# Two weight tiles instead of one follow each normed tile in five stages of a two-block model on one core

## The chip, the cores and the metric

The kernel runs on one core of a Trainium2 chip. The metric is the device time of one launch in microseconds (us). In three runs it was 3197.97, 3209.4 and 3214.88 us, median 3209.4.

## The reference, cut to what matters

A first block of two layers works on 256 context tokens and 512 latent tokens of width 1024 (a Hyena and mLSTM mixer, then latent attention, each followed by a convolved feed-forward); a second block (attention with a state-space mixer, then a mixture of experts) works on the 512 latent tokens. What the change touches are five products that follow an RMS norm:

```
y = xf * lax.rsqrt(jnp.mean(xf * xf, axis=-1, keepdims=True) + RMS_EPS)
...
u_ctx = h_ctx @ w_in                          # mixer of layer 0
...
g, u = jnp.split(h @ w_up, 2, axis=-1)        # feed-forward of either layer
...
return jnp.split(h @ w_down, [MLA_Q_RANK, MLA_Q_RANK + MLA_KV_RANK], axis=-1)
...
proj = h @ w_in[l]                            # second block, its q and k part
```

## The kernel before

Activations lie transposed: 8 tiles of 128 features (`DT` = 8, index `kk`) by 768 tokens, split in segments of 256 and 512 (`SEGS`), or 512 tokens alone (`SEG_LAT`). Every product is made in three passes (`three_passes`, lines 301 to 306): each float operand is split into a high part rounded to fp32r and a low part, and the matmuls high by high (L304), high by low (L305) and low by high (L306) are added in PSUM. So a weight tile of 128 output features takes 24 matmuls of 512 tokens, and 24 more of 256 tokens where there is context.

A weight tile comes through a `Stream` of two slots: SyncE loads it into `raw[s]`, ScalarE rounds the high part (`high`, L279), VectorE makes the low part (`low`, L283) and raises `ready[s]`. There is one pair of parts for each slot. So the high part of the tile after next can be written only when the product of this slot's tile is finished (`product[s]`), and this product needs `ready[s]` of its own tile and `taken[s]`, which says that its PSUM area has been read out. The work goes in turns of two tiles, p = 0 and p = 1. Turn 0 is written out by `from_first` and `in_spans`, the others are a hardware loop.

Five stages begin with a norm:

1. the Hyena projection (`project_conv`, 12 weight tiles, 768 tokens), called stage 1 below
2. the first feed-forward up (`ffn_up`, 22 tiles of gate and up side by side, 768 tokens), stage 2
3. the attention down projection (`project_act`, 6 tiles, 768 tokens), stage 3
4. the second feed-forward up (`ffn_up`, 22 tiles, 512 tokens), stage 4
5. the q and k projection of the second block (`project_act` with `NormOfNorm`, 6 tiles, 512 tokens), stage 5

The norm comes out tile by tile. For each kk VectorE scales x (L426, or L598 in stage 5), ScalarE applies gain and shift and rounds (L407 and L411, or L574 and L577), and VectorE makes the low part (L433, or L605) and raises `ready` of the norm. In stage 5 VectorE then writes x itself anew with 8 instructions of L611. In `project_as_normed` TensorE waits for each kk and runs the matmuls of one weight tile on it, both segments: tile p = 0 of turn 0 in stages 1, 3 and 5, and the gate half of tile p = 0 in stages 2 and 4. After the eighth normed tile comes the rest with `project`: all of tile p = 1 in stages 1, 3 and 5, the up half of tile p = 0 in stages 2 and 4 (p = 1 follows after it). `project` goes through all kk of a segment before the next segment.

After a product, ScalarE first rounds the slot's next weights (L279), then reads PSUM: L975 in `project_conv`, L1080 in `ffn_up`, L1552 in `project_act`. In `project_conv` VectorE then adds the outer taps out of PSUM (L1005, four instructions for each weight tile) and raises `taken`; in `project_act` L1552 raises it; in `ffn_up` the product of gate and up (L1122) does.

Of the kernel before, what the change touches and what calls it, by code (L numbers as in the profile page):

```python
# [31 lines left out]
P = 128  # L32
D = 1024
DT = D // P
# [266 lines left out]
def three_passes(k, out, stationary, moving, start, stop, **more):  # L301

    (sh, sl), (mh, ml) = stationary, moving
    k.nc.tensor.matmul(out, sh, mh, start=start, stop=False, **more)  # L304
    k.nc.tensor.matmul(out, sh, ml, start=False, stop=False, **more)  # L305
    return k.nc.tensor.matmul(out, sl, mh, start=False, stop=stop, **more)  # L306
# [26 lines left out]
            turn(i, False)  # L333


def project_as_normed(k, pe, norm, parts, psum_of, segs, col=0, width=P):

    for kk in range(DT):
        pe.wait_ge(norm.ready, kk + 1)
        at = kk * width + col  # L340
        for s, (t0, n) in enumerate(segs):
            last = three_passes(k, psum_of(s), [w[:, at:at + P] for w in parts], k.h_pair.tokens(kk, t0, t0 + n),
                                kk == 0, kk == DT - 1)
    return last


class Norm:
# [560 lines left out]
def project_conv(k, weights, dst, conv_w, conv_b, silu, taps=3, segs=SEGS, norm=None, then=None, also=(), begun=False):  # L908
    nc = k.nc
    k.stage()  # L910
    norm = Norm(k, *norm, segs, k.pair(2), k.bank(6), 7, begun) if norm else None
    stream = weights if isinstance(weights, Stream) else Stream(k, weights, D)
    tiles, turns = stream.tiles, stream.tiles // 2
    t0 = segs[0][0]
    product, taken = [k.sem("product0"), k.sem("product1")], [k.sem("taken0"), k.sem("taken1")]
    middle, summed, extra = k.sem("middle"), k.sem("summed"), k.sem("extra")
    offsets = [o - taps // 2 for o in range(taps) if o != taps // 2]
    per_tile = len(offsets) * len(segs)

    def sums(n, p):  # L920

        return k.arena[:, stream.at - (p + 1) * T:stream.at - p * T][:, t0:T] if silu else dst[:, n, :]

    with k.block() as block:
        @block.sync
        def _(sp):
            if also and not stream.ahead:
                stream.begin(sp)
            for place, array in also:
                sp.dma_start(place, array).then_inc(extra, 16)  # L930
            stream.load(sp, bool(also))
            if also:
                sp.wait_ge(extra, 16 * len(also))
            if then:
                then.begin(sp, stream)

        @block.tensor
        def _(pe):
            if norm:
                norm.sum_and_spread(pe)  # L940
            elif not stream.ahead:
                keep_running(k)

            def turn(i, first):
                for p in range(2):
                    psum_of = lambda s: k.pair(p)[:, segs[s][0]:segs[s][0] + segs[s][1]]
                    pe.wait_ge(stream.ready[p], i + (stream.base + 1))
                    pe.wait_ge(taken[p], i + 1)
                    if norm and first and p == 0:
                        last = project_as_normed(k, pe, norm, stream.parts[p], psum_of, segs)  # L950
                    else:
                        last = project(k, stream.parts[p], DT, k.h_pair, psum_of, segs)
                    last.then_inc(product[p], 1)

            from_first(pe, turns, turn)

        @block.scalar
        def _(act):
            if norm:
                norm.square(act)  # L960
            for p in range(0 if stream.ahead else 2):
                stream.high(act, p, 1)
            if norm:
                norm.shift(act)

            def turn(i, last):
                for p in range(2):
                    n = 2 * i + p
                    act.wait_ge(product[p], i + 1)
                    if not last:  # L970
                        stream.high(act, p, i + 2)
                    elif then:
                        then.high(act, p, 1)
                    bias = k.col(conv_b, n) if conv_b else 0.0
                    nc.scalar.activation(sums(n, p), k.pair(p)[:, t0:T], ACT.Identity,  # L975
                                         scale=k.col(conv_w, n + tiles * (taps // 2)), bias=bias).then_inc(middle, 1)
                    if silu:
                        act.wait_ge(summed, per_tile * (n + 1))
                        nc.scalar.activation(dst[:, n, :], sums(n, p), ACT.Silu)

            in_turns(act, turns, turn)

        @block.vector
        def _(dve):
            free_all(dve, taken)
            if norm:
                norm.add(dve)
            for p in range(0 if stream.ahead else 2):
                stream.low(dve, p, 1)
            if norm:  # L990
                norm.scale(dve)

            def turn(i, last):
                for p in range(2):
                    n = 2 * i + p
                    if not last:
                        stream.low(dve, p, i + 2)
                    elif then:
                        then.low(dve, p, 1)
                    dve.wait_ge(middle, n + 1)  # L1000
                    for m, o in enumerate(offsets):
                        for a, w in segs:
                            lo, hi = max(a, a - o), min(a + w, a + w - o)
                            out = sums(n, p)[:, lo - t0:hi - t0]
                            nc.vector.scalar_tensor_tensor(out=out, in0=k.pair(p)[:, lo + o:hi + o],  # L1005
                                                           scalar=k.col(conv_w, n + tiles * (o + taps // 2)), in1=out,
                                                           op0=ALU.mult, op1=ALU.add).then_inc(summed, 1)
                        dve.wait_ge(summed, per_tile * n + len(segs) * (m + 1))
                    nc.vector.sem_inc(taken[p], 1)

            in_turns(dve, turns, turn)
# [3 lines left out]
def ffn_up(k, layer, hidden, scratch, segs, norm, then, beside=None):  # L1015
    nc = k.nc
    k.stage()
    norm = Norm(k, *norm, segs, k.pair(3), k.bank(6), 5)
# [15 lines left out]
    with k.block() as block:  # L1034
# [6 lines left out]
        @block.tensor  # L1041
        def _(pe):
            norm.sum_and_spread(pe)

            def turn(i, kind):
                for p in range(2):
                    pe.wait_ge(stream.ready[p], i + (stream.base + 1))
                    pe.wait_ge(taken[p], i + 1)
                    gate_of = lambda s: gate(p, *segs[s])
                    up_of = lambda s: up(p)[:, segs[s][0]:segs[s][0] + segs[s][1]]  # L1050
                    if kind == "first" and p == 0:
                        project_as_normed(k, pe, norm, stream.parts[p], gate_of, segs, 0, 2 * P)
                    else:
                        project(k, stream.parts[p], DT, k.h_pair, gate_of, segs, 0, 2 * P)
                    project(k, stream.parts[p], DT, k.h_pair, up_of, segs, P, 2 * P).then_inc(product[p], 1)
                    if kind in ("sum both", "sum one"):
                        beside.sum(pe, i, p, kind == "sum both")

            in_spans(pe, ((0, 1, "first"),) + (((1, 2, ""), (2, 6, "sum both"), (6, 10, "sum one"), (10, turns, "")) if beside else ((1, turns, ""),)), turn)
# [429 lines left out]
def project_act(k, weights, dst, func, bias, segs, kt=DT, x=None, norm=None, then=None, also=(), first_norm=False):  # L1489
# [11 lines left out]
    with k.block() as block:  # L1501
# [12 lines left out]
        @block.tensor  # L1514
        def _(pe):
            if norm:
                norm.sum_and_spread(pe)
            elif not stream.ahead:
                keep_running(k)

            def turn(i, first):
                for p in range(2):
                    psum_of = lambda s: k.pair(p)[:, segs[s][0]:segs[s][0] + segs[s][1]]
                    pe.wait_ge(stream.ready[p], i + (stream.base + 1))
                    pe.wait_ge(taken[p], i + 1)
                    if norm and first and p == 0:
                        last = project_as_normed(k, pe, norm, stream.parts[p], psum_of, segs)
                    else:
                        last = project(k, stream.parts[p], kt, x, psum_of, segs)
                    last.then_inc(product[p], 1)  # L1530

            from_first(pe, turns, turn)

# [2277 lines left out]
```

## Time and profile before

| what | value |
|---|---|
| runs | 3197.97, 3209.4, 3214.88 us |
| span of the profiled execution | 3207.9 us |
| PE busy | 2924.0 us, 91% |
| DVE busy | 1710.8 us, 53% |
| ACT busy | 1207.4 us, 38% |
| mean granted TensorE clock | 0.957 |

No time is given for the profiled execution besides its span, from the first to the last instruction. PE is TensorE, DVE VectorE, ACT ScalarE, PEclk the granted TensorE clock with 1.00 for 2.4 GHz and 0.50 for 1.2 GHz. A share of busy time is a mean over all stages; what holds TensorE in one of them is read from the rows of that stretch.

### The profile page before, as it was taken

What the parts mean: (1) busy time and instruction counts of PE and PEld (TensorE: products, weight loads), DVE (VectorE), ACT (ScalarE), POOL (GpSimd) and SP (SyncE); (2) the same over time, 40 slices, a digit from 0 to 9 for tenths busy, and PEclk for the clock granted to TensorE, in tenths of its full rate; (3) what the DMA queues carried; (4) which work ended last, traced back from release to release, by engine and by line L of the source; (5) the groups of instructions that cost most, each with busy time, mean ns of one, the idle gap of its engine ahead of it and who ended that gap; (6) DMA issues with size and microseconds to landing.
All of it is one profiled execution on the core that took longest, in us unless ns stands there. A gap on an engine that the chain in (4) does not pass through costs nothing. (4 is left out here: it accounts for less than half of the span.)

```text
span 3207.9 us, 37971 instructions
## 1 busy us (share of the span) xinstructions
PE 2924.0 (91%) x14246; PEld 2331.5 (73%) x14246; DVE 1710.8 (53%) x2417; ACT 1207.4 (38%) x1619; POOL 166.6 (5%) x127
## 2 busy tenths in 40 slices
PE   7999989799999899898999999989878899899996
PEld 3774777678888798675777887867745677777775
DVE  7535323634767453435654433352366563788886
ACT  2320222424232242423334433244424432477774
POOL 0000001100011000000000000000000100122220
PEclk9999999899999999998999999999979998999998
DMA  8300110021345142110012221212200023799996
GB/s 367 131 20 13 53 53 2 27 92 56 122 147 174 66 151 98 53 37 27 1 34 85 94 102 66 95 62 85 79 8 1 1 66 122 277 360 363 353 347 238
DMA packets 76008, 362.79 MB, mean 113 GB/s; under 512 B 13170, under 2 KB 17043, under 8 KB 50292
## 3 DMA queue, kind: packets, MB, share of 16 engines
q1 hardware_dynamic: 62356, 327.66, 28.5%
q0 software_dynamic: 13536, 33.58, 3.1%
q8 instruction: 73, 1.20, 0.1%
q14 instruction: 43, 0.35, 0.0%
HBM read 360.67 MB, written 16.25 MB: 117 GB/s over the span
## 5 line engine op out<-in xcount | busy, mean ns | idle before, releaser
L304 PE MATMUL ps<-rounded,rounded 128*128 128x512 f32 (+3 forms) x3700 | 1381.6, 373 | 150.7 <-DVE rounded L2250 23.8
L305 PE MATMUL ps<-rounded,rounded 128*128 128x512 f32 (+3 forms) x3700 | 1340.8, 362 | 0.0
L306 PE MATMUL ps<-rounded,rounded 128*128 128x512 f32 (+3 forms) x3700 | 1338.9, 362 | 0.0
L304 PEld LDWEIGHTS ps<-rounded,rounded 128*128 128x128 f32 (+1 forms) x3700 | 707.8, 191 | 337.6 <-issue 112.4
L306 PEld LDWEIGHTS ps<-rounded,rounded 128*128 128x128 f32 (+1 forms) x3700 | 709.1, 192 | 107.9
L305 PEld LDWEIGHTS ps<-rounded,rounded 128*128 128x128 f32 (+1 forms) x3700 | 710.5, 192 | 95.3
L283 DVE TENSOR_TENSOR rounded<-work,rounded 128x1024 fp32r<-128x1024 f32 (+3 forms) x224 | 306.4, 1370 | 818.6 <-ACT rounded L279 818.4
L279 ACT CAST rounded<-work 128x1024 fp32r<-128x1024 f32 (+3 forms) x224 | 260.8, 1166 | 707.2 <-PE ps L306 612.1
L3562 DVE TENSOR_TENSOR rounded<-work,rounded 128x2048 fp32r<-128x2048 f32 x138 | 309.7, 2286 | 71.9 <-ACT rounded L3390 71.9
L3390 ACT CAST rounded<-work 128x2048 fp32r<-128x2048 f32 x138 | 259.1, 1913 | 77.9 <-PE ps L306 77.9
L290 PE MATMUL ps<-cst 128*128 128x256 f32 x566 | 147.3, 417 | 35.3 <-PEq L170 35.3
L290 PEld LDWEIGHTS ps<-cst 128*128 128x128 f32 x566 | 117.0, 212 | 59.9 <-issue 42.6
L279 ACT ACT_TABLE_LOAD x34 | 43.6, 1283 | 205.4 <-PE ps L306 196.3
L478 DVE SCALAR_TENSOR_TENSOR work<-work,silu_c 128x256 f32<-128x256 f32 x224 | 103.7, 484 | 14.1 <-DMA work<-in_ada_w 8.3
L2830 POOL TENSOR_TENSOR h<-work,row 128x2048 f32<-128x2048 f32 x2 | 8.2, 4100 | 1470.9 <-DVE h L2904 1470.9
L1005 DVE SCALAR_TENSOR_TENSOR work<-ps,vec,work 128x255 f32 (+4 forms) x116 | 72.5, 653 | 19.5 <-ACT work L975 13.6
L1083 ACT ACTIVATE work<-work 128x768 f32<-128x768 f32 (+1 forms) x44 | 32.5, 739 | 128.2 <-DVE work L1118 128.2
L2250 DVE TENSOR_TENSOR rounded<-ps,rounded 128x768 fp32r<-128x768 f32 (+1 forms) x64 | 52.3, 818 | 41.1 <-ACT rounded L2217 41.1
L1396 PE MATMUL ps<-work 128*128 128x512 f32 x160 | 71.6, 607 | 0.0
L3274 POOL DMA_INDIRECT y_rows<-h,whole x23 | 51.6, 2243 | 345.5 <-ACT h L3428 345.5
L2244 DVE TENSOR_REDUCE row<-ps 128x1 f32<-128x768 f32 (+1 forms) x64 | 52.5, 820 | 26.0 <-PE ps L306 25.8
L2210 ACT ACTIVATE x<-ps,row 128x768 f32<-128x768 f32 x32 | 28.9, 902 | 95.9 <-DVE row L2245 95.9
(487 smaller groups left out, 2483.8 us busy)
## 6 DMA issues: line engine op xcount, KB each, us to landing
work<-in_moe SPq DMA_DIRECT2D x138, 1024.0 KB, 7.4
work<-in_ffn_up SPq DMA_DIRECT2D x44, 1024.0 KB, 4.8
work<-in_ffn_down SPq DMA_DIRECT2D x66, 512.0 KB, 3.4
work<-in_ada_w SPq DMA_DIRECT2D x12, 2048.0 KB, 12.9
work<-in_ada_w POOLq DMA_DIRECT2D x48, 512.0 KB, 4.0
work<-in_w_out SPq DMA_DIRECT2D x16, 512.0 KB, 3.5
work<-in_w_gates SPq DMA_DIRECT2D x16, 512.0 KB, 3.5
work<-in_w_in_hy SPq DMA_DIRECT2D x12, 512.0 KB, 3.5
```

Of the source, the lines that this page charges most:

```text
L279: self.k.nc.scalar.copy(self.parts[s][0], self.raw[s]).then_inc(self.rounded[s], 1)
L283: self.k.nc.vector.tensor_tensor(self.parts[s][1], self.raw[s], self.high_plain[s], ALU.subtract).then_inc(self.ready[s], 1)
L290: k.nc.tensor.matmul(k.bank(bank, 2 * P), k.const("ident"), k.cst[:, 0:2 * P], start=True, stop=True)
L304: k.nc.tensor.matmul(out, sh, mh, start=start, stop=False, **more)
L305: k.nc.tensor.matmul(out, sh, ml, start=False, stop=False, **more)
L306: return k.nc.tensor.matmul(out, sl, mh, start=False, stop=stop, **more)
L478: done = self.k.nc.vector.scalar_tensor_tensor(out=total, in0=tile, scalar=by, in1=total, op0=ALU.mult, op1=ALU.add)
L1005: nc.vector.scalar_tensor_tensor(out=out, in0=k.pair(p)[:, lo + o:hi + o], scalar=k.col(conv_w, n + tiles * (o + taps // 2)), in1=out, op0 ...
L1396: last = nc.tensor.matmul(bank(group, part), tab[part][:, a, n * P:(n + 1) * P], src[:, a, :], start=a == 0, stop=a == count - 1)
L2244: chain.link(nc.vector.tensor_reduce(stats[:, b, 0:1], scores(u), AX.X, ALU.max))
L3390: nc.scalar.copy(ring.parts[:, c % ring.SPLIT, 0, :], ring.raw[c % ring.RAW]).then_inc(ring.rounded, 1)
L3562: V.tensor_tensor(ring.parts[:, s, 1, :], ring.raw[c % ring.RAW], ring.plain[:, s, 0, :], ALU.subtract).then_inc(ring.ready, 1)
```

## The change

`project_as_normed` takes a list of outputs and runs all of them on normed tile kk before it waits for kk + 1. Stages 1, 3 and 5 give it both tiles of turn 0, stages 2 and 4 gate and up of tile p = 0. `alone` is False for up, because up's 256 context tokens lie in the same PSUM bank as gate's: up must not start the accumulation there. Nothing else moves between engines, and the number of instructions is the same.

```diff
-def project_as_normed(k, pe, norm, parts, psum_of, segs, col=0, width=P):
+def project_as_normed(k, pe, norm, outs, segs, width=P):
...
     for kk in range(DT):
         pe.wait_ge(norm.ready, kk + 1)
-        at = kk * width + col
-        for s, (t0, n) in enumerate(segs):
-            last = three_passes(k, psum_of(s), [w[:, at:at + P] for w in parts], k.h_pair.tokens(kk, t0, t0 + n),
-                                kk == 0, kk == DT - 1)
-    return last
+        lasts = []
+        for parts, psum_of, col, alone in outs:
+            at = kk * width + col
+            for s, (t0, n) in enumerate(segs):
+                last = three_passes(k, psum_of(s), [w[:, at:at + P] for w in parts], k.h_pair.tokens(kk, t0, t0 + n),
+                                    kk == 0 and (alone or t0 > 0), kk == DT - 1, skip_group_check=True)
+            lasts.append(last)
+    return lasts
...
+                outs = []
                 for p in range(2):
-                    psum_of = lambda s: k.pair(p)[:, segs[s][0]:segs[s][0] + segs[s][1]]
+                    psum_of = lambda s, p=p: k.pair(p)[:, segs[s][0]:segs[s][0] + segs[s][1]]
                     pe.wait_ge(stream.ready[p], i + (stream.base + 1))
                     pe.wait_ge(taken[p], i + 1)
-                    if norm and first and p == 0:
-                        last = project_as_normed(k, pe, norm, stream.parts[p], psum_of, segs)
+                    if norm and first:
+                        outs.append((stream.parts[p], psum_of, 0, True))
                     else:
-                        last = project(k, stream.parts[p], DT, k.h_pair, psum_of, segs)
-                    last.then_inc(product[p], 1)
+                        project(k, stream.parts[p], DT, k.h_pair, psum_of, segs).then_inc(product[p], 1)
+                if outs:
+                    for p, last in enumerate(project_as_normed(k, pe, norm, outs, segs)):
+                        last.then_inc(product[p], 1)
...
                     if kind == "first" and p == 0:
-                        project_as_normed(k, pe, norm, stream.parts[p], gate_of, segs, 0, 2 * P)
+                        outs = [(stream.parts[p], gate_of, 0, True), (stream.parts[p], up_of, P, False)]
+                        project_as_normed(k, pe, norm, outs, segs, 2 * P)[1].then_inc(product[p], 1)
                     else:
                         project(k, stream.parts[p], DT, k.h_pair, gate_of, segs, 0, 2 * P)
-                    project(k, stream.parts[p], DT, k.h_pair, up_of, segs, P, 2 * P).then_inc(product[p], 1)
+                        project(k, stream.parts[p], DT, k.h_pair, up_of, segs, P, 2 * P).then_inc(product[p], 1)
```

The program of TensorE at the beginning of stage 1, before. `rounded_47616` and `rounded_48640` are the high and low part of weight tile 0, `rounded_49664` and `rounded_50688` those of weight tile 1, `rounded_18432` and `rounded_12288` the high and low part of the normed tiles, and even_10 is the norm's `ready`:

```order
L304 MATMUL ps<-rounded_18432_49,rounded_47616_51 128x256 [waits even_10,even_13,ready_ahead_00]
L305 MATMUL ps<-rounded_12288_50,rounded_47616_51 128x256
L306 MATMUL ps<-rounded_18432_49,rounded_48640_52 128x256
L304 MATMUL ps<-rounded_18432_49,rounded_47616_51 128x512
L305 MATMUL ps<-rounded_12288_50,rounded_47616_51 128x512
L306 MATMUL ps<-rounded_18432_49,rounded_48640_52 128x512
L304 MATMUL ps<-rounded_18432_49,rounded_47616_51 128x256 [waits even_10]
```

The same place with the change:

```order
L304 MATMUL ps<-rounded_18432_49,rounded_47616_51 128x256 [waits even_14,ready_ahead_01,even_10,even_13,ready_ahead_00]
L305 MATMUL ps<-rounded_12288_50,rounded_47616_51 128x256
L306 MATMUL ps<-rounded_18432_49,rounded_48640_52 128x256
L304 MATMUL ps<-rounded_18432_49,rounded_47616_51 128x512
L305 MATMUL ps<-rounded_12288_50,rounded_47616_51 128x512
L306 MATMUL ps<-rounded_18432_49,rounded_48640_52 128x512
L304 MATMUL ps<-rounded_18432_49,rounded_49664_53 128x256
L305 MATMUL ps<-rounded_12288_50,rounded_49664_53 128x256
L306 MATMUL ps<-rounded_18432_49,rounded_50688_54 128x256
L304 MATMUL ps<-rounded_18432_49,rounded_49664_53 128x512
L305 MATMUL ps<-rounded_12288_50,rounded_49664_53 128x512
L306 MATMUL ps<-rounded_18432_49,rounded_50688_54 128x512
```

Between two waits for the norm stand twelve matmuls instead of six, and the first of them waits for the second weight tile and its PSUM area too (ready_ahead_01, even_14).

The end of turn 0 of stage 1 with the change, TensorE again:

```order
L306 MATMUL ps<-rounded_18432_49,rounded_48640_52 128x512
L304 MATMUL ps<-rounded_18432_49,rounded_49664_53 128x256
L305 MATMUL ps<-rounded_12288_50,rounded_49664_53 128x256
L306 MATMUL ps<-rounded_18432_49,rounded_50688_54 128x256
L304 MATMUL ps<-rounded_18432_49,rounded_49664_53 128x512
L305 MATMUL ps<-rounded_12288_50,rounded_49664_53 128x512
L306 MATMUL ps<-rounded_18432_49,rounded_50688_54 128x512
L332 UNCONDITIONAL_BRANCH
L332 ISA
L304 MATMUL ps<-rounded_18432_49,rounded_47616_51 128x256 [waits even_13,ready_ahead_00]
```

The first row raises `product[0]`, and six matmuls later the loop begins with a wait for slot 0 (even_13 is `taken[0]`). Before, the 48 matmuls of weight tile 1 stood between the two.

VectorE's program in stage 5, the same before and with the change:

```order
L605 TENSOR_TENSOR rounded_12288_50<-h,rounded_18432_49 128x512 [waits odd_9] x2
L611 SCALAR_TENSOR_TENSOR x<-x,vec,ps 128x512 [waits odd_7]
L611 SCALAR_TENSOR_TENSOR x<-x,vec,ps 128x512 x7
L1565 UNCONDITIONAL_BRANCH
L1565 ISA
L283 TENSOR_TENSOR rounded_48640_52<-work,rounded_47616_51 128x1024 [waits odd_17]
```

The low part of weight tile 2 (L283) stands behind the eight instructions of L611.

## Rows read from the trace of the kernel before

**Rows 1.** The page: busy time (part 1); a weight load, KB, us to landing (part 6).
```profile
PE 2924.0 (91%) x14246; PEld 2331.5 (73%) x14246; DVE 1710.8 (53%) x2417; ACT 1207.4 (38%) x1619; POOL 166.6 (5%) x127
...
work<-in_w_in_hy SPq DMA_DIRECT2D x12, 512.0 KB, 3.5
```

**Rows 2.** Waits of PE from 736 to 1315 us: total, times, longest us.
```profile
PE ps L304 <- DVE rounded L1210: 8.5, 2, 8.3
```

**Rows 3.** DVE in stage 1, timeline: start us, us, instruction, [idle before <-releaser].
```profile
104.87 0.96 DVE L433 TENSOR_TENSOR rounded<-h,rounded 128x768 fp32r<-128x768 f32 x1 [1.37 <-ACT rounded L411]
...
119.39 0.96 DVE L433 TENSOR_TENSOR rounded<-h,rounded 128x768 fp32r<-128x768 f32 x1 [1.11 <-ACT rounded L411]
...
125.41 1.14 DVE L1005 SCALAR_TENSOR_TENSOR work<-ps,vec,work 128x255 f32 x2 [0.17 <-DVE work L1005]
```

**Rows 4.** PE in stage 1, timeline: first instruction of kk = 0, of weight tiles 1 and 2.
```profile
105.98 0.36 PE L304 MATMUL ps<-rounded,rounded 128*128 128x256 f32 x1 [1.00 <-DVE rounded L433]
...
121.57 0.27 PE L304 MATMUL ps<-rounded,rounded 128*128 128x256 f32 x1
...
129.90 0.28 PE L304 MATMUL ps<-rounded,rounded 128*128 128x256 f32 x1
```

**Rows 5.** Stage 2, timelines of PE (kk = 0; weight tile 1) and DVE.
```profile
721.13 0.36 PE L304 MATMUL ps<-rounded,rounded 128*128 128x256 f32 x1 [1.37 <-DVE rounded L433]
...
734.55 0.96 DVE L433 TENSOR_TENSOR rounded<-h,rounded 128x768 fp32r<-128x768 f32 x1 [1.12 <-ACT rounded L411]
...
745.05 0.28 PE L304 MATMUL ps<-rounded,rounded 128*128 128x256 f32 x1
...
753.98 0.95 DVE L1122 TENSOR_TENSOR work<-work,ps 128x768 f32<-128x768 f32 x1 [0.91 <-ACT work L1083]
```

**Rows 6.** Stage 3, timelines of DVE and PE (weight tiles 1 and 2).
```profile
1344.94 0.96 DVE L433 TENSOR_TENSOR rounded<-h,rounded 128x768 fp32r<-128x768 f32 x1 [1.11 <-ACT rounded L411]
...
1347.12 0.27 PE L304 MATMUL ps<-rounded,rounded 128*128 128x256 f32 x1
...
1348.48 1.23 DVE L283 TENSOR_TENSOR rounded<-work,rounded 128x1024 fp32r<-128x1024 f32 x1 [2.59 <-ACT rounded L279]
...
1355.44 0.28 PE L304 MATMUL ps<-rounded,rounded 128*128 128x256 f32 x1
```

**Rows 7.** Stage 4, timelines of DVE and PE (up half; weight tile 1).
```profile
1742.43 0.69 DVE L433 TENSOR_TENSOR rounded<-h,rounded 128x512 fp32r<-128x512 f32 x1 [0.68 <-ACT rounded L411]
...
1743.99 0.40 PE L304 MATMUL ps<-rounded,rounded 128*128 128x512 f32 x1
...
1749.47 0.39 PE L304 MATMUL ps<-rounded,rounded 128*128 128x512 f32 x1
```

**Rows 8.** Stage 5, timelines of DVE and PE (weight tile 2).
```profile
2145.58 0.69 DVE L605 TENSOR_TENSOR rounded<-h,rounded 128x512 fp32r<-128x512 f32 x1 [0.59 <-ACT rounded L577]
2146.19 5.35 DVE L611 SCALAR_TENSOR_TENSOR x<-x,vec,ps 128x512 f32<-128x512 f32 x8
2151.46 1.22 DVE L283 TENSOR_TENSOR rounded<-work,rounded 128x1024 fp32r<-128x1024 f32 x1
...
2152.73 0.50 PE L304 MATMUL ps<-rounded,rounded 128*128 128x512 f32 x1
```

**Rows 9.** PE timeline: three pauses elsewhere, in brackets before the instruction.
```profile
217.29 1.08 PE L1362 MATMUL ps<-work 33*64 33x512 f32 x1 [3.83 <-PEq L170]
...
515.14 0.29 PE L304 MATMUL ps<-rounded,rounded 128*16 128x256 f32 x1 [3.42 <-DVE rounded L1989]
...
1671.27 0.50 PE L304 MATMUL ps<-rounded,rounded 128*128 128x512 f32 x1 [3.05 <-DVE rounded L283]
```

**Rows 10.** After those pauses: stretch, us, PE busy (x), PEclk, DMA share, GB/s.
```profile
217.30:223.10 5.80, 5.80 (x20) 0.55 0.00 0
...
515.20:523.20 8.00, 8.00 (x40) 0.79 0.00 0
...
1671.30:1679.30 8.00, 8.00 (x35) 1.00 0.40 132
```

More of the change, by code:

```diff
@@ L1521, in turn @@
             def turn(i, first):
+                outs = []
                 for p in range(2):
-                    psum_of = lambda s: k.pair(p)[:, segs[s][0]:segs[s][0] + segs[s][1]]
+                    psum_of = lambda s, p=p: k.pair(p)[:, segs[s][0]:segs[s][0] + segs[s][1]]
                     pe.wait_ge(stream.ready[p], i + (stream.base + 1))
                     pe.wait_ge(taken[p], i + 1)
-                    if norm and first and p == 0:
-                        last = project_as_normed(k, pe, norm, stream.parts[p], psum_of, segs)
-                    else:
-                        last = project(k, stream.parts[p], kt, x, psum_of, segs)
-                    last.then_inc(product[p], 1)
+                    if norm and first:
+                        outs.append((stream.parts[p], psum_of, 0, True))
+                    else:
+                        project(k, stream.parts[p], kt, x, psum_of, segs).then_inc(product[p], 1)
+                if outs:
+                    for p, last in enumerate(project_as_normed(k, pe, norm, outs, segs)):
+                        last.then_inc(product[p], 1)
             from_first(pe, turns, turn)
```

## The prediction, made before the changed kernel ran

> **What bounds the kernel now.** I read the page first, for the share of each engine: TensorE is busy 91% of the span [rows 1]. That is a mean and doesn't say what a stage is worth, so next I read the waits of TensorE. From the first normed tiles of stage 2 to the end of its feed-forward there is in essence one, of 8.3 us, at the entry to the down projection [rows 2]. So what TensorE gains early in such a stage reaches its end. Last I read the timelines of the five passes over the normed tiles. In stage 1 VectorE finishes a normed tile every (119.39 - 104.87) / 7 = 2.07 us [rows 3]. A weight tile of 48 matmuls takes TensorE 129.90 - 121.57 = 8.33 us, 1.04 us for each normed tile [rows 4]. While it has one weight tile to run, TensorE therefore stands still for half of the pass: the norm (VectorE and ScalarE) bounds it. After the pass TensorE bounds the stage.
>
> **The pass.** The change puts 2 x 1.04 = 2.08 us of matmuls on each normed tile that comes every 2.07 us. The pass then ends about when it ended before plus one share of the second output. It is reckoned from the last normed tile: its end, 0.15 us until TensorE starts (105.98 after 104.87 + 0.96) [rows 3, 4], and 2.08 us. With 512 tokens the share is (1749.47 - 1743.99) / 8 = 0.685 us, two are 1.37 us [rows 7]. No matmul is added or dropped, so all that counts is when TensorE starts on the next weight tile, against before.
>
> Stage 2: the pass ends at 734.55 + 0.96 + 0.15 + 2.08 = 737.7. Gate and up of tile 0 are then both done, and the next weight tile, whose weights are ready and whose PSUM is free, starts there in place of 745.05 [rows 5]: **7.3 us** gained. Its successor needs slot 0 again, whose last user L1122 ends 753.98 + 0.95 - 745.05 = 9.9 us after the product. Weight tile 1 (gate and up) covers that with 2 x 8.33 = 16.7 us, as it did before; without that cover the difference would be a wait.
>
> Stage 4: 1742.43 + 0.69 + 0.15 + 1.37 = 1744.6 in place of 1749.47 [rows 7]: **4.8 us**. The cover of the next slot is the same one, 2 x 5.48 us here.
>
> Stages 1, 3 and 5 give both slots to the pass, and this adds a wait. `product[0]` comes when it came before, one share before the end of the pass, but TensorE has 1.04 us of work behind it where it had 8.33. Then it stands before weight tile 2, which needs slot 0 to be refilled and its PSUM read. Behind that wait is all of the stage.
>
> Stage 3: before, product 0 was done at 1347.12 and the low part of weight tile 2 at 1348.48 + 1.23 = 1349.71 [rows 6]. L1552, which frees the PSUM, runs beside it on ScalarE. TensorE starts at 1349.9 in place of 1355.44: **5.6 us** gained, with a pause of 1.7 us after the end of the pass at 1348.1.
>
> Stage 1: here the PSUM is freed only after four L1005, at 125.41 + 1.14 = 126.55 [rows 3]. With the passing on of two semaphores I take 126.8, in place of 129.90: **3.1 us** gained, and a pause of 4.2 us from 122.6 on.
>
> Stage 5: VectorE has eight L611 ahead of the low part of weight tile 2, from 2146.19 to 2151.5, and the low part is done at 2152.68. TensorE started on weight tile 2 at 2152.73, at once after weight tile 1 [rows 8]. That start hangs on VectorE alone, so **nothing** is gained: the second weight tile was the cover of L611, and is now done at 2145.58 + 0.69 + 0.15 + 1.37 = 2147.8. A pause of 4.9 us takes its place.
>
> The weights of turn 1 cost nothing: SyncE asks for them as soon as those of turn 0 are rounded, before the normed tiles come, over 15 us ahead. Should a load be late, it costs up to its landing, 3.5 us [rows 1].
>
> Sum so far: 3.1 + 7.3 + 5.6 + 4.8 + 0 = 20.8 us.
>
> **The clock.** Two long pauses of TensorE are new, 4.2 and 4.9 us. The trace has such pauses elsewhere [rows 9, 10]. After one of 3.83 us the granted clock was 0.55 over 5.8 us, so 5.8 x 0.45 = 2.6 us of work were lost. After one of 3.42 us it was 0.79 over 8 us: 1.7 us lost. After one of 3.05 us it stayed at 1.00. The bounds are thus 0 and 2.6 us for each; the new pauses are longer than both that cost something, so I take the middle of these, 2.1 us, twice 4.2 us. The pause of 1.7 us in stage 3 is well below the one that cost nothing, and I give it nothing. The other two stages have no new pause.
>
> The Trainium skill has a rule that speaks against this change: by "TensorE: Matmul & The Clock Gate", section "Why this matters for your kernels", idle gaps of more than about 3 us between bursts of matmuls put the clock back to the lower level. By it both pauses cost, and the sum is 20.8 - 4.2 = 16.6 us; without it the sum is 20.8 us. This trace agrees for 3.42 and 3.83 us, while its gap of 3.05 us went unpunished.
>
> The profiled span is 3207.9 us, 1.5 us under the median of the three runs. I put the difference on the median: 3209.4 - 16.6 = **3192.8 us**.
>
> **The rivals.**
>
> Clock kept: neither pause costs, as after 3.05 us [rows 10]. 3209.4 - 20.8 = 3188.6 us. Against it stand the two longer pauses.
>
> Clock dearer: each long pause costs 2.6 us, and the one of 1.7 us in stage 3 costs 1.7 us as well. 20.8 - 6.9 = 13.9 us, 3195.5 us. For it: the new pauses are longer than the one that cost 2.6 us [rows 9, 10], and stage 3 has its pause right after a pass with no idle time. Against it: 1.7 us is little over half of the pause that cost nothing.
>
> Given back: a gain of an early stage is waited away later, where a transfer or another engine bounds. If only the feed-forwards keep theirs, 12.1 - 4.2 = 7.9 us are left, 3201.5 us; if nothing does, 3209 us. Against it: after stage 2 TensorE waits for no DMA [rows 2].
>
> The other side: TensorE runs the combined pass at 1.2 GHz. Then 2.08 us become 4.16 and the norm no longer bounds. Eight of them are 33.3 us: stage 2 would start its next weight tile at 721.13 + 33.3 = 754.4, 9.4 us late [rows 5], and stages 1 and 3, whose passes are as long, about as late with their pauses of 4.2 and 1.7 us on top, 13.6 and 11.1 us. Stages 4 and 5, with 8 x 2.74 = 21.9 us, would be about 6 us late each. Together some 46 us: 3255 us. Each us at the half clock costs 0.5 us, so it decides from 2 x 16.6 = 33 us of half clock in the five passes, which last 3 x 16.7 + 2 x 11 = 72 us. Against it: weight tiles that run without pauses take 8.33 us, which is the full clock [rows 4].
>
> That the change doesn't do what it says is excluded by the order of the instructions: twelve matmuls stand between two waits for the norm, where six stood.
>
> **How the numbers follow.** Forecast 0.50, clock kept 0.13, clock dearer 0.20, given back 0.12, the other side 0.05. A measurement of this kernel can tell about 0.5% from no change, 16.0 us, so the line lies at 3193.4 us, just beside the forecast. The three runs shown spread over 17 us, so a median may lie 4 us off. Of the forecast I give half to each side (0.27 faster), of the clock kept 0.11, of the dearer clock 0.07, of given back 0.01. Faster 0.46, within 0.5% 0.49, slower 0.05. The range takes in clock kept and clock dearer with those 4 us, and half of given back: 3184 to 3205 us.
>
> **What would show it.** In stages 2 and 4 the first matmul of weight tile 1 about 24 and 16 us after the first matmul on a normed tile would be wrong; right are about 16.6 and 11 us. In stage 1 TensorE should wait some 4 us for L1005 or its semaphore before weight tile 2, in stage 3 1.7 us for L283, and in stage 5 4.9 us for L283 behind L611, with weight tile 2 no earlier against the first normed tile than before. The granted clock should read about 0.8 in the 8 us after the pauses of stages 1 and 5, and 1.00 in the passes. The prediction is wrong if the pass runs slower than 2.1 us for each normed tile, if stage 5 gains, or if later waits grow by what was won.

## The result, and the profile after

Over the 6 runs of each that belong to this comparison the changed kernel takes 3196.68 us (3187.7 to 3202.01) and the kernel before 3212.18 us (3197.97 to 3223.89). The ratio is 0.9945, with an interval of 0.9922 to 0.9968: 0.55% faster, some 17.7 us of 3212 by the ratio (the two medians lie 15.5 us apart). The profiled execution has a time of 3196.56 us and a span of 3194.7 us.

The stages are best read from marks inside the program, since the opening alone differs between executions, as is shown further down. The mark of a stage is its first matmul on a normed tile. With the change the lines stand 5 to 12 lower: L438 is the low part of a normed tile, L1013 the taps, L610 the low part in stage 5, L616 x anew.

Stage 1, the timeline of TensorE; the stage begins at 108.61:

```profile
108.61 0.36 PE L304 MATMUL ps<-rounded,rounded 128*128 128x256 f32 x1 [1.43 <-DVE rounded L438]
...
125.26 0.39 PE L306 MATMUL ps<-rounded,rounded 128*128 128x512 f32 x1
...
129.63 0.55 PE L304 MATMUL ps<-rounded,rounded 128*128 128x256 f32 x1 [3.97 <-DVEq L1017]
```

Weight tile 2 starts 21.0 us after the mark, where it was 23.9 [rows 4]. The new wait is there, 3.97 us, and what ended it is the semaphore behind VectorE's taps (L1017 raises `taken`). VectorE at the same place:

```profile
125.80 1.22 DVE L283 TENSOR_TENSOR rounded<-work,rounded 128x1024 fp32r<-128x1024 f32 x1 [2.80 <-ACT rounded L279]
126.97 1.14 DVE L1013 SCALAR_TENSOR_TENSOR work<-ps,vec,work 128x255 f32 x2
128.28 1.14 DVE L1013 SCALAR_TENSOR_TENSOR work<-ps,vec,work 128x255 f32 x2 [0.17 <-DVE work L1013]
129.57 1.23 DVE L283 TENSOR_TENSOR rounded<-work,rounded 128x1024 fp32r<-128x1024 f32 x1
```

The weights of weight tile 2 are ready at 127.0. It is the last taps, ending at 129.42, that TensorE waits for.

Stage 2, TensorE has no pause after the mark:

```profile
722.90 0.36 PE L304 MATMUL ps<-rounded,rounded 128*128 128x256 f32 x1 [1.38 <-DVE rounded L438]
...
739.58 0.39 PE L306 MATMUL ps<-rounded,rounded 128*128 128x512 f32 x1
739.80 0.28 PE L304 MATMUL ps<-rounded,rounded 128*128 128x256 f32 x1
```

The pass, gate and up together, takes 739.80 - 722.90 = 16.9 us where the two took 23.92 [rows 5]. In stage 4 it takes 1737.91 - 1726.80 = 11.1 us:

```profile
1726.80 0.58 PE L304 MATMUL ps<-rounded,rounded 128*128 128x512 f32 x1
...
1737.91 0.39 PE L304 MATMUL ps<-rounded,rounded 128*128 128x512 f32 x1
```

Before it took 16.05 us, from its mark to the row at 1749.47 [rows 7]. The marks of stages 3, 4 and 5 in the kernel before:

```profile
1331.53 0.36 PE L304 MATMUL ps<-rounded,rounded 128*128 128x256 f32 x1 [1.74 <-DVE rounded L433]
...
1733.42 0.47 PE L304 MATMUL ps<-rounded,rounded 128*128 128x512 f32 x1
...
2136.76 0.47 PE L304 MATMUL ps<-rounded,rounded 128*128 128x512 f32 x1 [1.33 <-DVE rounded L605]
```

Stage 3, and stage 5 behind it, the timeline of TensorE:

```profile
1326.05 0.36 PE L304 MATMUL ps<-rounded,rounded 128*128 128x256 f32 x1 [1.74 <-DVE rounded L438]
...
1342.70 0.39 PE L306 MATMUL ps<-rounded,rounded 128*128 128x512 f32 x1
1344.52 0.39 PE L304 MATMUL ps<-rounded,rounded 128*128 128x256 f32 x1 [1.43 <-DVE rounded L283]
...
2126.68 0.47 PE L304 MATMUL ps<-rounded,rounded 128*128 128x512 f32 x1 [1.33 <-DVE rounded L610]
...
2137.62 0.40 PE L306 MATMUL ps<-rounded,rounded 128*128 128x512 f32 x1
2142.65 0.80 PE L304 MATMUL ps<-rounded,rounded 128*128 128x512 f32 x1 [4.64 <-DVE rounded L283]
```

VectorE in stage 5:

```profile
2136.11 5.35 DVE L616 SCALAR_TENSOR_TENSOR x<-x,vec,ps 128x512 f32<-128x512 f32 x8
2141.38 2.35 DVE L283 TENSOR_TENSOR rounded<-work,rounded 128x1024 fp32r<-128x1024 f32 x2
```

In stage 3 weight tile 2 starts 18.5 us after the mark at 1326.05, where it was 1355.44 - 1331.53 = 23.9 [rows 6]. In stage 5 it starts 15.97 us after the mark at 2126.68, and it was 2152.73 - 2136.76 = 15.97 us too [rows 8]: TensorE waits 4.64 us for the low part that stands behind x anew.

The clock, by stretches of the changed kernel (us, PE busy (x), PEclk, DMA share, GB/s):

```profile
108.61:125.33 16.72, 16.72 (x96) 1.00 0.54 180
129.70:137.70 8.00, 8.00 (x35) 0.64 0.22 72
722.90:739.50 16.60, 16.60 (x95) 1.00 0.00 1
1326.05:1342.80 16.75, 16.75 (x96) 1.00 0.00 1
1344.50:1352.50 8.00, 7.98 (x46) 1.00 0.43 133
1726.00:1737.20 11.20, 11.20 (x50) 1.00 0.01 1
2126.70:2137.90 11.20, 11.20 (x48) 1.00 0.00 0
2142.70:2150.70 8.00, 8.00 (x29) 0.80 0.41 133
```

All five passes run at 2.4 GHz without a pause. After the two long pauses the clock is lower over the next 8 us, after the short one in stage 3 it is not. The kernel before has 1.00 over the 8 us from the start of weight tile 2 in all of stages 1, 3 and 5.

### The profile page after: what moved, and what is told of

Its sections match the earlier page's. It is cut to its first block and busy times, and to the rows that moved or that the text cites. A ratio compares the mean times of both kernels' runs of the same rounds, so it can differ in the third digit from the quotient of the medians.

```text
span 3194.7 us, 37971 instructions
## 1 busy us (share of the span) xinstructions
PE 2921.8 (91%) x14246; PEld 2337.4 (73%) x14246; DVE 1710.3 (54%) x2417; ACT 1207.7 (38%) x1619; POOL 166.6 (5%) x127
## 5 line engine op out<-in xcount | busy, mean ns | idle before, releaser
L283 DVE TENSOR_TENSOR rounded<-work,rounded 128x1024 fp32r<-128x1024 f32 (+3 forms) x224 | 306.2, 1370 | 801.7 <-ACT rounded L279 801.5
L279 ACT CAST rounded<-work 128x1024 fp32r<-128x1024 f32 (+3 forms) x224 | 260.6, 1166 | 702.0 <-PE ps L306 601.2
L290 PE MATMUL ps<-cst 128*128 128x256 f32 x566 | 150.2, 424 | 35.3 <-PEq L170 35.3
L290 PEld LDWEIGHTS ps<-cst 128*128 128x128 f32 x566 | 118.9, 216 | 60.7 <-issue 42.6
L1013 DVE SCALAR_TENSOR_TENSOR work<-ps,vec,work 128x255 f32 (+4 forms) x116 | 72.4, 653 | 19.5 <-ACT work L983 13.6
```

Of the source, the lines that this page charges most:

```text
L279: self.k.nc.scalar.copy(self.parts[s][0], self.raw[s]).then_inc(self.rounded[s], 1)
L283: self.k.nc.vector.tensor_tensor(self.parts[s][1], self.raw[s], self.high_plain[s], ALU.subtract).then_inc(self.ready[s], 1)
L290: k.nc.tensor.matmul(k.bank(bank, 2 * P), k.const("ident"), k.cst[:, 0:2 * P], start=True, stop=True)
```

## The experiments

Each kernel was timed against the kernel before on the same chip, in three sets that share their runs of it. Unless said otherwise a kernel computes everything.

The first set asks what each part of the change is worth, and what the pauses cost.

**The change again** (`whole`; no edit).

> The change as it is, again, beside the other three. Theory A (local gains, less the clock): 3.1 + 7.3 + 5.6 + 4.8 us won at the passes, some 4 us lost to the clock after the pauses of stages 1 and 5, about 16 to 18 us under the kernel before, ratio 0.9945 to 0.995. Theory B (the clock is luck of the execution and the local gains are all that counts): 20.8 us, ratio 0.9935. In the trace: the stretch from the first normed matmul to weight tile 2 again 21.0 us in stage 1 and 16.0 us in stage 5.

Measured: 3195.39 us against 3211.0, ratio 0.9949 (0.993 to 0.9967).

**The feed-forwards alone** (`ffn_only`). Stages 1, 3 and 5 have the old pass; the cut shows stage 1 (`project_conv`), and the same is done in `project_act` for stages 3 and 5:

```diff
-                    if norm and first:
-                        outs.append((stream.parts[p], psum_of, 0, True))
+                    if norm and first and p == 0:
+                        project_as_normed(k, pe, norm, [(stream.parts[p], psum_of, 0, True)], segs)[0].then_inc(product[p], 1)
```

> Only stages 2 and 4 have the new pass, stages 1, 3 and 5 have the old one. Theory A: no new pause, so no loss to the clock, and 7.3 + 4.8 = 12.1 us under the kernel before, ratio 0.9962, with 16.9 us from the first normed matmul to the next weight tile in stage 2 and 11.2 us in stage 4. Theory C (the feed-forwards carry the whole gain and the projections give theirs back to the clock): ratio equal to that of the whole change, about 0.9945.

Measured: 3199.14 us, ratio 0.9966 (0.9947 to 0.9985), some 11 us. The value of theory A, 0.9962, is in the interval, that of theory C, 0.9945, lies just below it. Stages 1 and 3 run the code of the kernel before, but in this profile they took 112.03 and 60.12 us (table below), 0.7 and 1.5 us more than before. In stage 3 the granted clock fell at the end of the old pass (us, PE busy (x), PEclk, DMA share, GB/s):

```profile
1341.40:1344.90 3.50, 3.50 (x14) 0.51 0.00 0
```

**The projections alone** (`proj_only`). Stages 2 and 4 have the old pass:

```diff
-                        outs = [(stream.parts[p], gate_of, 0, True), (stream.parts[p], up_of, P, False)]
-                        project_as_normed(k, pe, norm, outs, segs, 2 * P)[1].then_inc(product[p], 1)
+                        project_as_normed(k, pe, norm, [(stream.parts[p], gate_of, 0, True)], segs, 2 * P)
+                        project(k, stream.parts[p], DT, k.h_pair, up_of, segs, P, 2 * P).then_inc(product[p], 1)
```

> Only stages 1, 3 and 5 have the new pass. Theory A: 3.0 + 5.5 + 0 us won, less about 4 us of clock after the pauses of stages 1 and 5: 4 to 5 us under the kernel before, ratio 0.9985. Theory C: nothing or a loss, ratio 1.000 or above. Theory B: 8.5 us, ratio 0.9974. The clock over the 8 us after the pauses should read about 0.65 and 0.8, and 1.00 in stage 3.

Measured: 3206.29 us, ratio 0.9978 (0.996 to 0.9997), some 7 us. That the projections give all back (theory C) falls; between theories A and B the interval doesn't decide, but the trace does. The 8 us after the pauses of stages 1, 5 and 3 (us, PE busy (x), PEclk, DMA share, GB/s):

```profile
128.80:136.80 8.00, 7.96 (x37) 0.70 0.24 79
2151.40:2159.40 8.00, 8.00 (x29) 0.82 0.35 133
1350.00:1358.00 8.00, 7.96 (x46) 1.00 0.38 133
```

Stage 1 takes 110.58 us, stage 3 53.26 and stage 5 42.19 us (table below), so 0.7 + 5.3 - 1.3 = 4.7 us are won, which is theory A.

**The pauses filled** (`kept_warm`). TensorE runs idle matmuls (L290), whose result nobody reads, where it stood: 8 in stage 1 and 9 in stage 5. The trace shows each of them as two. The comments in this cut name the functions:

```diff
                         last.then_inc(product[p], 1)
+                    keep_running(k, 8, 7)              # project_conv
...
+                    if first_norm:                     # project_act
+                        keep_running(k, 9, 6)
```

> The whole change, and in the pauses of stages 1 and 5 TensorE runs 8 and 9 idle matmuls on an unused PSUM bank. Theory A: the clock reads 1.00 over the 8 us after both pauses, weight tile 2 starts no later, and the kernel is 3 to 5 us under the whole change, ratio to the kernel before about 0.993. Rival: the clock falls in these places whatever TensorE does in the pause, or falls later elsewhere by as much, and the time is that of the whole change.

Measured: 3194.45 us, ratio 0.9944 (0.9925 to 0.9963), 1 us under `whole` of the same set, where theory A had 3 to 5. The measurement can't tell 1 us from nothing or from 3 us, so the launch times don't exclude the rival that the clock is paid for elsewhere. The trace tells more. Its timeline of TensorE in stage 1 and at the stage's end, and the clock over the 8 us after both pauses:

```profile
128.42 3.61 PE L290 MATMUL ps<-cst 128*128 128x256 f32 x16
132.55 0.35 PE L304 MATMUL ps<-rounded,rounded 128*128 128x256 f32 x1 [0.52 <-DVEq L1018]
...
220.00 1.08 PE L1372 MATMUL ps<-work 33*64 33x512 f32 x1 [3.82 <-PEq L170]
```

```profile
132.50:140.50 8.00, 7.95 (x46) 1.00 0.22 77
2138.90:2146.90 8.00, 8.00 (x35) 1.00 0.37 131
```

The mark of this execution is 111.55. Weight tile 2 starts 21.0 us after it, as before, and the stage ends (first matmul of the next one) after 108.45 us, against 111.1 us with the change as it is (108.61 to 219.70) and 111.3 us in the kernel before (105.98 to the row at 217.29 [rows 9]). So the clock after the pause costs stage 1 what the earlier start wins, and it is the pause that brings it down. Stage 5 takes 40.83 us, the time of the kernel before, where `whole` has 43.63.

The second set undoes the two pauses, or leaves these stages alone.

**x anew later** (`late_x`). VectorE makes the low parts of weight tiles 2 and 3 first; the eight instructions are moved out of `scale` into `keep_x`:

```diff
                 norm.scale(dve)
-            with dve.Fori(1, turns) as i:
+            if first_norm:
+                for p in range(2):
+                    stream.low(dve, p, 2)
+                norm.keep_x(dve)
+            with dve.Fori(2 if first_norm else 1, turns) as i:
```

> The whole change, and in stage 5 VectorE makes the low parts of weight tiles 2 and 3 before it writes x anew (the eight L611). Theory A (the start of weight tile 2 hangs on VectorE's queue alone): weight tile 2 starts 13.1 us after the first normed matmul instead of 15.97, the pause shrinks from 4.6 to below 2 us and the clock reads 1.00 after it, so that the whole stage (first normed matmul to the first one of the next stage) takes 38 us instead of 42.2 to 43.6, and the kernel is some 5 us under the whole change: ratio 0.993. Rival (the start hangs on ScalarE's rounding or on the PSUM as well): no change of the 15.97 us.

Measured: 3194.73 us against 3208.43, ratio 0.9954 (0.9937 to 0.997).

The timelines of VectorE and TensorE in stage 5:

```profile
2136.05 1.23 DVE L283 TENSOR_TENSOR rounded<-work,rounded 128x1024 fp32r<-128x1024 f32 x1 [2.32 <-ACT rounded L279]
...
2137.33 0.50 PE L304 MATMUL ps<-rounded,rounded 128*128 128x512 f32 x1 [1.80 <-DVE rounded L283]
```

The mark is 2124.21: weight tile 2 starts 13.1 us after it, as theory A has it, and the pause is 1.80 us. So in the change the start hung on VectorE's queue; now the low part waits for ScalarE's rounding of the high part (L279). But the clock fell all the same in the 8 us behind it:

```profile
2137.30:2145.30 8.00, 7.97 (x28) 0.79 0.46 133
```

The stage took 39.6 us, not 38. Theory A was wrong in that a pause of under 2 us would be free; this rests on one profile. In time the gain over the change isn't seen: this set has no run of the change itself, and the ratio lies within the interval of `whole`.

**Three stages** (`three_stages`). Stages 2, 3 and 4 have the new pass, stages 1 and 5 the old one, by the same edit as in `ffn_only`.

> The new pass in stages 2, 3 and 4 only; stages 1 and 5 have the old one. Theory A (stages 1 and 5 give to the clock what they win, or more): 7.1 + 5.3 + 4.8 = 17.2 us under the kernel before, ratio 0.9946, the same as the whole change or 1 to 2 us under it. Rival (the new pass is worth its 3 us in stage 1 in spite of the clock): 3 us slower than the whole change, ratio 0.9955.

Measured: 3197.37 us, ratio 0.9969 (0.9955 to 0.9983), 11 us under the kernel before in place of 17. The value of theory A, 0.9946, is outside of the interval, and the rival's, 0.9955, is its lower end. The trace has what the theory wants in every one of the five stages (111.3, 53.2 and 40.9 us in stages 1, 3 and 5, table below), and its span, 3188.0 us, is the third shortest of all. But this execution was the fastest of twelve (3189.79 to 3205.46 us), so its span says little of the median. So the sum over the stages and the measured times disagree here by some 6 us, and this is open. By the launch times alone it isn't shown that the new pass is worth nothing in stage 1.

**The second weight tile lags** (`lagged`). As `late_x`, and in the pass the second output leaves out the last 4 (stage 1), 2 (stage 3) and 3 (stage 5) normed tiles until the first output is done:

```diff
+    for kk in range(DT):
+        pe.wait_ge(norm.ready, kk + 1)
+        run(0, kk)
+        if kk < DT - lag:
+            run(1, kk)
+    for kk in range(DT - lag, DT):
+        run(1, kk)
```

> As late_x, and the second weight tile of the pass leaves the last 4, 2 and 3 normed tiles (stages 1, 3, 5) until the first weight tile is finished, so that these matmuls lie where the pause was. Theory A: no pause of more than about 1 us after the pass, weight tile 2 starts at the same distance from the first normed matmul (21.0, 18.5, 13.1 us), the clock reads 1.00 over the next 8 us, stage 1 takes 108.4 us from its first normed matmul to its end instead of 110.6 to 111.1, and the kernel is 22 to 23 us under the kernel before: ratio 0.993. Rival: the idle time of TensorE, now spread over the last normed tiles, lets the clock fall there as in the kernel before at 117 us, and the time is that of late_x or above.

Measured: 3190.39 us, ratio 0.9946 (0.9926 to 0.9966), 18 us under the kernel before, where theory A had 22 to 23. The timeline of TensorE in stage 1 (mark 108.63) and at its end, and the clock from the end of its pass on and after weight tile 2 begins in stages 1, 3 and 5:

```profile
121.00 0.39 PE L304 MATMUL ps<-rounded,rounded 128*128 128x256 f32 x1 [0.77 <-DVE rounded L446]
...
123.07 0.38 PE L304 MATMUL ps<-rounded,rounded 128*128 128x256 f32 x1 [0.76 <-DVE rounded L446]
...
129.41 0.36 PE L304 MATMUL ps<-rounded,rounded 128*128 128x256 f32 x1 [0.83 <-DVEq L1028]
...
216.86 1.21 PE L1382 MATMUL ps<-work 33*64 33x512 f32 x2 [3.83 <-PEq L170]
```

```profile
124.50:129.40 4.90, 4.08 (x23) 1.00 0.28 84
129.40:137.40 8.00, 7.99 (x47) 1.00 0.26 82
1341.20:1349.20 8.00, 8.00 (x47) 1.00 0.42 133
2133.00:2141.00 8.00, 7.99 (x35) 1.00 0.43 133
```

Weight tile 2 starts 20.8 us after the mark. The idle time up to it stands in four pieces of 0.60, 0.77, 0.76 and 0.83 us, 3.0 us together where it was one of 3.97, the clock stays, and stage 1 takes 108.2 us. That it is the spreading that keeps the clock, and not the 1 us less of idle time, is not isolated.

**Both, by filling** (`late_x_warm`). `late_x` with 8 idle matmuls in stage 1 and 2 in stage 5.

> As late_x, with idle matmuls on an unused bank in the pause of stage 1 (8) and stage 5 (2). Theory A: the same stage times as lagged (108.4 us in stage 1, 38 us in stage 5), ratio 0.993. Rival (the clock then falls elsewhere in the same measure): the time of late_x.

Measured: 3190.89 us, ratio 0.9944 (0.9923 to 0.9965), the time of `lagged` within the noise, with 108.5 and 38.0 us in stages 1 and 5. Both are some 4 us under `late_x` of the same set (3194.73 us); the intervals of the ratios overlap.

The third set measures the best one against the change, with a control.

> The lagged version once more, on the same chip as the whole change. Its stretches in the first profile were 108.23, 53.04 and 37.87 us in stages 1, 3 and 5, against 110.75, 53.25 and 43.63 us with the whole change, 8.5 us less in sum. Theory A: ratio to the kernel before 0.992 to 0.994, and 5 to 8 us under the whole change. Rival (the first call's ratio was all there is): 2 us or less under it.

Measured: 3189.51 us against 3207.91, ratio 0.9938 (0.9919 to 0.9958).

> The change as it is, third measurement: 16 to 18 us under the kernel before by theory A, ratio 0.995; the same stretches of 21.0, 16.6, 18.5 and 16.0 us from the first normed matmul to the next weight tile in stages 1, 2, 3 and 5.

Measured: 3196.03 us, ratio 0.9962 (0.9948 to 0.9976).

> The kernel before under another name, as a control: ratio 1.000, with an interval of about 0.002 on either side, and in its profile 111.3, 58.6 to 60.1 and 40.9 us in stages 1, 3 and 5, while stretches that the change doesn't touch differ by several us from the other profiles.

Measured: 3208.6 us, ratio 0.9998 (0.9987 to 1.0009).

In this set the lagged version is 6.5 us under the change, as theory A had it (5 to 8 us), though the intervals of the two ratios just overlap. It has the lowest median in both of its sets; in the second `late_x_warm` equals it.

The stretches of all profiles, in us: from the mark of a stage to the first matmul of the next one (stages 1, 3, 5), from the mark of stage 2 to that of stage 3, from the mark of stage 4 to that of stage 5; and three that none of the kernels touches.

```
                opening  stage 1  2 to 3  stage 3  4 to 5  stage 5 | 1 to 2   3 to 4   after 5
before           105.98   111.31  610.40   58.59   403.34   40.87  | 503.84   343.30   1030.27
control          109.03   111.30  609.98   58.60   403.83   40.83  | 502.83   345.17   1029.03
changed          108.61   111.09  603.15   53.25   399.88   42.42  | 503.20   347.50   1025.60
whole            111.57   110.75  603.19   53.25   396.21   43.63  | 502.84   341.61   1033.25
whole_again      108.86   111.18  603.16   53.28   399.63   43.74  | 503.41   344.76   1029.48
ffn_only         110.23   112.03  603.18   60.12   399.59   40.87  | 501.42   345.01   1026.15
proj_only        107.82   110.58  610.22   53.26   403.68   42.19  | 502.94   346.92   1029.59
kept_warm        111.55   108.45  602.92   53.26   399.50   40.83  | 503.63   343.62   1031.84
late_x           108.52   110.85  602.20   53.24   398.41   39.61  | 501.98   349.01   1025.98
three_stages     104.67   111.30  603.10   53.22   396.10   40.85  | 501.68   345.13   1031.95
lagged           108.63   108.23  603.06   53.04   399.98   37.87  | 503.00   344.07   1027.62
lagged_again     107.95   108.26  602.77   53.01   399.98   37.88  | 502.11   347.51   1025.93
late_x_warm      111.47   108.48  604.42   53.25   398.46   38.00  | 503.27   344.26   1030.09
```

## Why the prediction was right

Forecast were 3192.8 us, 16.6 us under the median before; measured were 3196.68 us. The median before is itself 2.8 us higher with more runs, and three measurements of the change gave 0.9945, 0.9949 and 0.9962, which are 12 to 18 us. Point by point, with the table:

- **The pass.** Two outputs on a normed tile of 2.07 us, at the full clock, ended when predicted: 16.9 us in stage 2 (16.6 predicted), 11.1 to 11.3 us in stage 4 (11.2). The 0.3 us in stage 2 are the size of the share: 16.9 / 8 = 2.11 us for the twelve matmuls of a normed tile where I had 2.08, a little over the norm's pace of 2.07, so that TensorE and no longer the norm sets the pass by a hair.
- **Stage 2, 7.3 us.** Right: 610.2 (mean of before, control and `proj_only`) to 603.1 us, 7.1 us.
- **Stage 4, 4.8 us.** Right: 403.6 to a mean of 398.8 us over the ten profiles with the new pass in it, though single ones differ by 4 us. Up to the first matmul of the second block's norm (L554; L559 or L567 in the others) it takes 390.9 to 392.2 us in the three profiles with the old pass and 386.6 to 387.3 in the ten with the new one, 4.4 us less in the mean. In the kernel before that matmul stands at 2125.60, 392.18 us after the mark, in the changed one at 2113.84, 387.04 us after it.
- **Stage 3, 5.6 us.** Right: 58.6 to 53.25 us, 5.35. The pause is 1.43 us, and the clock stays.
- **Stage 1, 3.1 us, less 2.1 for the clock.** The start is 2.9 us earlier, ended by the semaphore behind the taps, as said. The clock costs 110.9 (mean of the five profiles with the pause) less 108.45 with the pause filled, 2.4 us. Of the stage's gain 0.4 us is left (111.3 to 110.9).
- **Stage 5, nothing, less 2.1 for the clock.** Right in both: 15.97 us to weight tile 2 with either kernel, and 42.2 to 43.7 us for the stage, a mean of 43.0 in the four profiles with the pause, against 40.85: a loss of 2.1 us. That the mean falls on the forecast is partly luck, since single profiles lost 1.3 to 2.9 us and the 2.1 were the middle of two costs read elsewhere.
- **The sum** of what the stages show is 7.1 + 4.8 + 5.35 + 0.4 - 2.1 = 15.5 us. The mean of the three ratios, 0.9952, is 15.4 us of 3209. So close an agreement is partly luck too, with intervals of 0.003 to 0.005 around each ratio.

Of the rivals, the clock kept and the other side fell with the granted clock (0.62 to 0.70 and 0.61 to 0.82 after the pauses, 1.00 in the passes). That the gain is given back later fell with the table: the three stretches that no kernel touches take 503.3, 344.2 and 1029.7 us in the mean of the kernel before and its control, and 502.7, 345.4 and 1028.9 in that of the other eleven. The dearer clock was half right: stage 1 paid 2.1 to 2.7 us, near the upper bound; stage 3 paid nothing.

What the prediction had too narrow is the noise around the sum. I put it at 4 us for a median and gave the clock's part to the two pauses alone. The table shows where the rest is: in the opening (104.7 to 111.6 us), in "3 to 4" (341.6 to 349.0) and in "after 5" (1025.6 to 1033.3), none of which any kernel here touches. In "3 to 4" the trace points to the clock again. The changed kernel's profile has

```profile
1651.00:1663.00 12.00, 9.82 (x34) 0.57 0.27 89
```

while `whole`, the same program, has at that point of the work

```profile
1647.00:1659.00 12.00, 7.63 (x46) 1.00 0.24 78
```

and takes 5.9 us less for the stretch. Over the whole stretch the shortest of all profiles (`whole`, first row) and the longest (`late_x`) have the clocks:

```profile
1381.60:1723.21 341.61, 314.13 (x1565) 0.96 0.12 40
```

```profile
1376.79:1725.80 349.01, 322.06 (x1565) 0.93 0.12 39
```

The number of matmuls is the same, and TensorE is idle for 27 us in either. Why the clock differs between executions there is not shown.

With such swings a gain of 2 us in one stage is seen in its trace and not in the time.

## What to carry to other kernels

Where a producer paces a matrix engine that is half idle, give the engine the next piece of work on the same operand: each stage wins nearly that piece's time. But look first at what that piece had been hiding. If it covered the refill of the next slot, a PSUM read-out or another engine's chores, the wait comes out. Here one of the five stages won only 0.4 us and another lost 2.1 us for that reason, until the chores were moved back and the idle time was broken up or filled. Judge gains of some us by marks inside the program, not by the launch.

## What was not expected of the hardware

The same placement of pauses costs different amounts. After a pause of 3.97 us in stage 1 the clock read 0.62 to 0.70 over 8 us in five profiles; after one of 4.64 us in stage 5 it read 0.80, 0.82, 0.63 and 0.61 in four. The two rows of `whole_again`, stages 1 and 5:

```profile
129.86:137.86 8.00, 8.00 (x35) 0.62 0.21 74
2140.25:2148.25 8.00, 8.00 (x22) 0.61 0.42 133
```

A pause of 1.80 us in `late_x` was followed by 0.79, while one of 1.43 us in stage 3 was followed by 1.00 in all eight profiles that have it, and one of 3.05 us in the kernel before too [rows 9, 10]. Some 3.0 us of idle time in pieces of 0.6 to 0.8 us left the clock up in stage 1 of `lagged`. But small pieces are no safeguard: in the old pass of the kernel before TensorE stood for 0.70 to 0.77 us in each 2.07 us, and after the fifth of these pieces its clock fell:

```profile
116.70:120.00 3.30, 3.19 (x11) 0.50 0.00 0
```

There it cost nothing: the stage took 111.31 us, and 111.30 in the control, whose clock stayed at 1.00 in this pass. The same fall, later in the old pass, in stage 3 of `ffn_only` went with a stage that was 1.5 us longer. What decides between these cases no run here isolates. By the Trainium skill, "TensorE: Matmul & The Clock Gate", section "Why this matters for your kernels", gaps of more than about 3 us put the clock back; the 1.80 us here speak against taking that as a safe bound for shorter ones, and the 3.05 us against taking it as a certain loss.
